# Cross sums of a residual norm: ScalarE's second square replaced by a multiply with squared gains on VectorE

## The reference

```python
def rmsnorm_2(x, g):
    xf = x.astype(jnp.float32)
    y = xf * lax.rsqrt(jnp.mean(xf * xf, axis=-1, keepdims=True) + RMS_EPS)
    return (y * g.astype(jnp.float32)).astype(x.dtype)
...
        h = h + rmsnorm_2(m, g[1])
        u = rmsnorm_2(h, g[2])
        h = h + rmsnorm_2(swiglu(u, ffn_w_gate[layer], ffn_w_up[layer], ffn_w_down[layer]), g[3])
```

## Time and profile before

| | |
|---|---|
| median of 3 runs | 1730.98 us (1729.67 to 1731.14) |
| the profiled execution, its own time | 1730.87 us |
| its span in the trace | 1729.2 us |
| PE busy | 1675.1 us, 97% of the span |
| DVE busy | 903.0 us, 52% |
| ACT busy | 626.2 us, 36% |
| mean granted TensorE clock | 0.981 of full speed |

### The profile page before, as it was taken

One profiled execution on the slowest core, in us unless ns is written; L12 is line 12 of the kernel. 1 busy time (PEld: TensorE's weight loads), 2 busy tenths in 40 slices (PEclk: granted clock), 3 DMA queues, 4 the chain that ended last, 5 costly groups with the idle time before them and its releaser, 6 DMA issues.

```text
span 1729.2 us, 22141 instructions
## 1 busy us (share of the span) xinstructions
PE 1675.1 (97%) x8311; PEld 1328.1 (77%) x8311; DVE 903.0 (52%) x1361; ACT 626.2 (36%) x930; POOL 208.5 (12%) x197
## 2 busy tenths in 40 slices
PE   5999999999999999999999999999998999999996
PEld 4667788888888867777776888888887688888885
DVE  6756765444334473766667444444337644444223
ACT  2224443323223262655555333333226433333221
POOL 1101008997000030000000000003000000000000
PEclk9999999999999999999999999999998899999998
DMA  9573224554333241111111322233211222223221
GB/s 364 175 220 107 87 85 161 190 172 146 110 101 100 78 112 62 50 37 50 38 46 34 128 97 97 97 105 106 100 41 49 81 94 94 97 96 124 100 67 49
DMA packets 48589, 179.28 MB, mean 104 GB/s; under 512 B 5969, under 2 KB 6641, under 8 KB 48273
## 3 DMA queue, kind: packets, MB, share of 16 engines
q1 hardware_dynamic: 43600, 162.04, 27.6%
q0 software_dynamic: 3776, 14.78, 2.8%
q10 hardware_dynamic: 1152, 1.66, 0.4%
HBM read 173.04 MB, written 2.10 MB: 101 GB/s over the span
## 4 chain that ended last, share of the span: by engine, by line
PE 71%; issue 22%; DVE 4%; DMA 1%; ACT 1%; SPq 1%; POOL 0%; ACTq 0%; POOLq 0%; DVEq 0%
PE bank L396 15%; PE bank L397 15%; PE bank L398 15%; PE bank L1494 3%; PE bank L1496 2%; PE bank L1495 2%; PE bank L1602 2%; PE bank L1558 2%; PE bank L1577 1%; PE bank L1268 1%; PE bank L1220 1%; DMA conv<-in_ada_w 1%; PE bank L1666 1%; PE bank L1222 1%; PE bank L1221 1%
## 5 line engine op out<-in xcount | busy, mean ns | idle before, releaser
L322 DVE TENSOR_TENSOR w_lo<-raw,w_hi 128x1024 fp32r<-128x1024 f32 (+1 forms) x229 | 313.6, 1370 | 581.4 <-ACT w_hi L318 581.2
L318 ACT ACTIVATE w_hi<-raw 128x1024 fp32r<-128x1024 f32 (+1 forms) x229 | 258.0, 1127 | 568.2 <-PE bank L398 487.8
L396 PE MATMUL bank<-h_hi,w_hi 128*128 128x512 f32 x1136 | 449.1, 395 | 0.5 <-DVE w_lo L322 0.5
L397 PE MATMUL bank<-h_lo,w_hi 128*128 128x512 f32 x1136 | 443.3, 390 | 0.0
L398 PE MATMUL bank<-h_hi,w_lo 128*128 128x512 f32 x1136 | 443.0, 390 | 0.0
L396 PEld LDWEIGHTS bank<-h_hi,w_hi 128*128 128x128 f32 x1136 | 213.8, 188 | 50.6 <-issue 5.4
L397 PEld LDWEIGHTS bank<-h_lo,w_hi 128*128 128x128 f32 x1136 | 213.9, 188 | 44.9 <-issue 1.7
L398 PEld LDWEIGHTS bank<-h_hi,w_lo 128*128 128x128 f32 x1136 | 213.9, 188 | 44.8
L396 PE MATMUL bank<-hid_hi,w_hi 128*128 128x512 f32 x528 | 205.6, 389 | 0.0
L397 PE MATMUL bank<-hid_lo,w_hi 128*128 128x512 f32 x528 | 205.4, 389 | 0.0
L398 PE MATMUL bank<-hid_hi,w_lo 128*128 128x512 f32 x528 | 205.4, 389 | 0.0
(11 more groups left out here) (414 smaller groups left out, 2049.6 us busy)
## 6 DMA issues: line engine op xcount, KB each, us to landing
raw<-in_f2i SPq DMA_DIRECT2D x88, 512.0 KB, 3.3
raw<-in_ffi SPq DMA_DIRECT2D x44, 512.0 KB, 3.4
raw<-in_f2o SPq DMA_DIRECT2D x32, 704.0 KB, 4.0
ada_w<-in_ada_w SPq DMA_DIRECT2D x24, 512.0 KB, 4.6
m_out<-in_ada_w POOLq DMA_DIRECT2D x24, 512.0 KB, 3.7
raw<-in_att_w SPq DMA_DIRECT2D x23, 512.0 KB, 3.3
raw<-in_ffo SPq DMA_DIRECT2D x16, 704.0 KB, 4.1
raw<-in_w_in SPq DMA_DIRECT2D x16, 512.0 KB, 6.0
```

Of the source, the lines that this page charges most:

```text
L318: nc.scalar.activation(WH[par][:, 0:kc * P], RAW[s][:, 0:kc * P], ACT.Copy).then_inc(whi, count)
L322: nc.vector.tensor_tensor(WL[par][:, 0:kc * P], RAW[s][:, 0:kc * P], WH[par][:, 0:kc * P].bitcast(F32), ALU.subtract).then_inc(wlo, count)
L396: pe_.matmul(bank[:, :], w_h, hi[:, k0 + k, :], start=start and k == 0, stop=False)
L397: pe_.matmul(bank[:, :], w_h, lo[:, k0 + k, :], start=False, stop=False)
```

## The change

The gained square (g*m) squared equals m squared times g squared, and m squared is in TMP already. POOL computes the squared gains once, early, into a small new tile GSQ (called `gain_squares`), three times 128x8. DVE's addition to SMM becomes one scalar_tensor_tensor: TMP times the chunk's column of GSQ, plus SMM. ACT's third pass over the bank goes in all three stages, 24 activations in all, and TMM is no longer written there. The bank is released by the gained copy. In the pool stage chunk 0 had its gained square written straight to SMM; now a tensor_scalar on DVE makes it from ACC.

TMP[:, b] now has two readers on DVE, so ACT waits with the first square of chunk m until SMM holds chunk m - 2. In `act_m` that wait was there, for chunk m - 1, and is now for m - 2; in the pool stage it moves from the third activation to the first.

The new tile takes 96 bytes of each partition, and moves what is allotted behind it by as much.

```diff
@@ (act_m)
             if js is not None:
-                nc.scalar.wait_ge(n_mms, 9 * js + m + 1)
+                nc.scalar.wait_ge(n_mms, 9 * js + m)
             nc.scalar.activation(TMP[:, b, :], PS[b][:, :], ACT.Square).then_inc(n_sq, 1)
-            into = nc.scalar.activation(M[:, bass.ds(m, 1), :], PS[b][:, :].rearrange("p (a s) -> p a s", a=1),
-                                        ACT.Copy, scale=gain)
-            if js is None:
-                into.then_inc(ev[b], 1)
-            else:
-                nc.scalar.activation(TMM[:, b, :], PS[b][:, :], ACT.Square, scale=gain).then_inc(ev[b], 1)
+            nc.scalar.activation(M[:, bass.ds(m, 1), :], PS[b][:, :].rearrange("p (a s) -> p a s", a=1),
+                                 ACT.Copy, scale=gain).then_inc(ev[b], 1)
@@ (dve_cross)
-            nc.vector.tensor_tensor(SMM, SMM, TMM[:, b, :], ALU.add).then_inc(n_mms, 1)
+            nc.vector.scalar_tensor_tensor(SMM.rearrange("p (a s) -> p a s", a=1), TMP[:, b:b + 1, :],
+                                           GSQ[:, js - 1, bass.ds(m, 1)], SMM.rearrange("p (a s) -> p a s", a=1),
+                                           ALU.mult, ALU.add).then_inc(n_mms, 1)
@@ (POOL, behind conv_tiles)
+            for j in range(3):
+                gain_ = VEC[:, COL["norm_g2"] + 16 * j + 8:COL["norm_g2"] + 16 * j + 16]
+                chain(pool.tensor_tensor(GSQ[:, j, :], gain_, gain_, ALU.mult))
@@ (pool_squares)
                     act.wait_ge(n_acc, nj["r3"].acc + o)
+                    act.wait_ge(n_mms, 27 + o)
                 act.activation(ACC if o == 0 else TMP[:, b, :], PS[b][:, :], ACT.Square,
                                scale=vcol("pool_s", o)).then_inc(n_sq, 1)
-                act.activation(M[:, o, :], PS[b][:, :], ACT.Copy, scale=PG[:, o:o + 1])
-                if o >= 2:
-                    act.wait_ge(n_mms, 27 + o)
-                act.activation(SMM if o == 0 else TMM[:, b, :], PS[b][:, :], ACT.Square,
-                               scale=PG[:, o:o + 1]).then_inc(ev[b], 1)
+                act.activation(M[:, o, :], PS[b][:, :], ACT.Copy, scale=PG[:, o:o + 1]).then_inc(ev[b], 1)
@@ (pool_sums, chunk 0)
+                    dve.wait_ge(n_sq, nj["r3"].sq + 1)
+                    dve.tensor_scalar(SMM, ACC, GSQ[:, 2, 0:1], None, ALU.mult).then_inc(n_mms, 2)
                     dve.sem_inc(n_acc, 2)
-                    dve.sem_inc(n_mms, 2)
@@ (pool_cross)
-                dve.tensor_tensor(SMM, SMM, TMM[:, b, :], ALU.add).then_inc(n_mms, 1)
+                dve.scalar_tensor_tensor(SMM, TMP[:, b, :], GSQ[:, 2, o:o + 1], SMM, ALU.mult, ALU.add).then_inc(n_mms, 1)
```

More of the change, by code:

```diff
@@ L106, in build_program @@
         PG = sb("pool_gs", [P, C])
+        GSQ = sb("gain_squares", [P, 3, C])
         CACT = sb("c_act", [P, C])
```

## The result

The changed kernel is slower. Its median is 1743.2 us (1741.75 to 1744.59, 4 runs), that of the kernel before in the same comparison 1730.33 us (1727.07 to 1731.14, 4 runs): ratio 1.0078, 95% interval 1.0066 to 1.0091, or 12.9 us. 1730.3 was forecast. The profiled execution took 1743.68 us, its span 1742.0.

What follows compares the result with a forecast made beforehand. PE, busy 97% of the span, was taken as the bound. Start of att_out -0.37, its end +0.06 and pool stage -0.32 us sum to -0.63, giving 1730.3 us; range 1728.3 to 1732.3.

Steps and rivals of the forecast that it cites:

- the sum: The three stages' terms added, -0.37 + 0.06 - 0.32 = -0.63 us, giving 1730.3 us.
- The 96 bytes by which tiles move: Tiles behind GSQ: the move was taken as free, with half a us either way put into the range.
- the clock's two sides: PE's clock around the pool stage's end: falling sooner gives 1732.3 us, holding longer and returning sooner 1728.2.
- a difference that sits ... in a stage without changed code: Sign named beforehand that would show the forecast wrong, as would a difference in the granted clock.
- Start of att_out: PE at block 2 waits for w_lo instead of ACT's third square: -0.37 us, bounds 0 and 0.58.
- The new addition: DVE's scalar_tensor_tensor into SMM: a step of 0.66 us instead of 0.603, +0.06 us each.
- DVE takes it back: Rival, att_out's end and pool stage: the addition costs 0.78 us, leaving -0.28 us in all, 1730.6; chance 0.10.
- Pool stage: Chunk 4's product starts 0.44 us earlier, two additions cost 0.12: -0.32 us, bounds 0 and -0.44.
- Ends of the stages: DVE's last sums behind the diagonal: +0.06 us in att_out, 0 in ffo1 and the pool stage, hidden by the lower clock.
- The two rivals: PE's clock around the pool stage's end: slower clock, 1732.3 us, chance 0.15; better clock, 1728.2 us, chance 0.15.
- Their 3 us for the clock's return: In L467 after the pool stage, full clock back 3 us later or sooner: 1.3 us lost or gained.

Runs made afterwards that it cites:

- e1: Kernel before with 96 unused bytes where the change puts GSQ, none of the changed code: 1742.03 us.
- e3: Changed kernel with 160 unused bytes behind GSQ, so that later tiles move by 256 in all: 1728.81 us, ratio 0.9997 to the kernel before.
- e7: Kernel before with 32 unused bytes ahead of all its tiles, weights included: 1731.74 us, ratio 1.0007.
- e9: Kernel before with the 32-byte tile GL moved ahead of the weights; weights and h move by 32, hid, ao and conv stay: 1744.21 us.
- f3: Changed kernel padded to 256 bytes, with ACT's third square put back only to release the bank: 1733.11 us in one run.
- e8: Kernel before with 32 unused bytes ahead of the split weights and 32 behind them: 1764.84 us, ratio 1.02.
- f1: Kernel before with 32 unused bytes ahead of w_lo and 224 behind it, so only w_lo is off: 1764.06 us in one run.
- f2: Kernel before with 32 unused bytes ahead of h_lo and 224 behind it, so only h_lo is off: 1750.21 us in one run.

## Why the prediction was wrong

**The step that failed** is the last sentence of the sum: "The 96 bytes by which tiles move have no price in any row; I take nothing for them, and half a us either way into the range". They cost about all of the 12.9 us: e1 has the bytes alone and lost 12.1 (1742.03 against 1729.91 in its own comparison), e3 has the change with the distances at 0 and lost nothing. The price was bounded by half a us without a row for it. No row of one trace could have given it, since every split operand stood at distance 0; but then the bound was a guess and not a result, and the range of 1728.3 to 1732.3 rested on it. (That range holds not even the half us: the clock's two sides alone, 1728.2 and 1732.3, fill it. And 1729.6 to 1731.1, called the spread of the three runs shifted by the terms, is that spread unshifted.) What could have been seen is how much work the moved tiles carry: 640 triples, three matmuls each, all on the engine that is busy 97%. A price of 1% on the 680 ns of a triple is already 4.4 us there, and the one measured is 3%. The prediction did name what would show it wrong, "a difference that sits ... in a stage without changed code", and it sits there: by the first `ao` matmul 4.8 us are lost, before any changed instruction of the three stages has run.

**Start of att_out**, forecast -0.37: right in kind, a little large. The releaser is `w_lo` as said, with 1.20 us of idle in e3 for 1.1 forecast (1.16 in the changed kernel): -0.29. PE started 0.14 us after the end of L324 (889.27 against 887.90 + 1.23 = 889.13), not 0.05 as behind ACT.

**The new addition**, forecast +0.06: right. Its groups of the changed kernel, against the earlier trace rows:

```profile
L718 DVE SCALAR_TENSOR_TENSOR h_scratch<-tmp,gain_squares,h_scratch 128x512 f32<-128x512 f32 x16 | 12.1, 755 | 0.0
...
L2614 DVE SCALAR_TENSOR_TENSOR h_scratch<-tmp,gain_squares,h_scratch 128x512 f32<-128x512 f32 x7 | 5.2, 743 | 0.0
```

743 and 755 ns, near L779's 743 and far from the 864; in e3 one starts at 1328.55 and the next instruction 0.66 us later (1329.21). "DVE takes it back" falls, and with it the row that spoke for it: the group at 864 has 745 in the changed kernel, so 864 wasn't the price of the form.

**Pool stage**, forecast -0.32: 5.69 against 6.00 is -0.31, and both parts came as forecast: the product starts 0.43 us sooner behind the ACC sum (0.61 for 1.04), and from it to chunk 6's ACC sum it takes 4.34 us for 4.22. DVE no longer idles ahead of chunk 4's product, PE stands 2.71 us ahead of its sum as forecast (2.7), and ACT's first square of chunk 7 waits for DVE's addition as said (1.20 us) without PE waiting for it: it ended at 1332.56, ahead of L527 at 1333.93.

**Ends of the stages**, forecast +0.06 in att_out: not seen. In e3 DVE's last sum ended at 926.91 + 0.68 = 927.59, and the matmuls of L545 started only at 928.25, 1.87 us behind the broadcast (L533, 926.38), as they do in the pool stage at the lower clock. The granted clock had fallen to 0.50 ahead of that broadcast in e3; it fell 0.24 us into it in the changed kernel, and 0.72 us into it in the kernel before, where L543 started straight behind DVE's sum. So the 0.06 was hidden. From the first sum to the first L467 (L469 in e3) att_out's end took 9.02 us before and 9.52 in e3, more than that term and due to the clock: e1, e7 and e9, with the old code, have 9.52 too.

**The clock.** From the first sum on PE in the pool stage to DVE's L553 (L554 after, L555 in e3 and f3) it is 2.90 us before, 3.32 after, 2.39 in e3 and 2.95 in f3. In the changed kernel the clock fell during L522, 0.35 us behind its start:

```profile
1344.05 1.57 PE L522 MATMUL bank<-ones,tmp 128*128 128x1 f32 x8 [2.71 <-DVE tmp L2604]
...
1345.48 1.84 PE L526 MATMUL bank<-ones,tmp 128*128 128x1 f32 x8
```

In e3 the same two groups took 1.05 and 1.44 us after the same 2.71 us of idle; there the clock fell 1.37 us behind the start. So that idle time doesn't decide it alone. Nor does the change: in the nine kernels with the old code and moved tiles the same stretch took 2.22 to 3.61 us. The two rivals named a spread that is there with and without the change, and no run shows that the change moves it. Their 3 us for the clock's return came from no row. In the changed kernel and in e3 the stretch at 0.50 lasted 13.7 us as before, so the clock returned half a us sooner or later, as it had fallen. In e8, f1 and f2, with the old code, it lasted 17.1 us, so that a return 3 us later does occur.

With the tiles in place the sum of -0.63 us would have been right as far as runs can tell: e3 is 0.5 us below the kernel before, inside an interval of -2.2 to +1.2 us (0.9987 to 1.0007 of 1729.31). Local gains of 0.29 and 0.31 are seen in the traces; that they reach the end isn't shown.

**What stays open** is why the distance counts. A PE that loads the next weights while it streams the current operand reads two tiles at once (PEld was busy 33.10 of 40 us beside a PE that never stood), and two reads whose addresses meet differently would fit. The shares within a triple in f1 and f2 point the same way, but no run here took the loads and the streams apart. That distances of 64 are cheaper, and 160 a little dearer, isn't explained either. Not tried: `h_hi` or `w_hi` alone off, 512-column matmuls of other types, other widths, and steps finer than 32 bytes.

## What to carry to other kernels

A new tile moves all that is allotted behind it; when it moves an operand of the engine that bounds the kernel, build the old code with the same unused bytes first, so that address and code are told apart. In this kernel a new small tile is to be rounded up to 256 bytes (or put behind everything else), so that weights and moving operands of split matmuls keep the same start modulo 256. And a term "without a price in any row" on the bounding engine belongs into the range with the number of instructions that it touches times some per cent of each, not with half a us. Here it was 3% of a triple.

## What the runs showed of the hardware

- A triple of fp32r matmuls of 128x512 took 680 ns with all four tiles at the same start modulo 256 bytes of a partition, and 700 ns with both moving tiles 32, 96, 128, 192 or 224 bytes off those of the weights; 686.7 at 64 and 702.8 at 160. `w_lo` alone or `h_lo` alone off by 32 cost the same 20 ns. The granted clock was 1.00 in these stretches.
- For a kernel with 1976 such triples this is 12 to 13 us (640 of them off) to 35 us (all), 0.7 to 2%.
- The rest modulo 256 by itself is free: with everything moved by 32 the ratio was 1.0007 (0.9997 to 1.0017).
- A scalar_tensor_tensor of 128x512 with two fp32 tiles took 743 to 755 ns on DVE in these stages, a tensor_tensor 682 to 700, a tensor_scalar with one tile 481 (e3, L2600).
